# The softmax's division moved into the product that turns the probabilities

## The reference, cut to what matters

```python
s_loc = jnp.einsum('bnqkgd,bskd->bkgnqs', qb, kw).astype(jnp.float32) * scale
s_ctx = jnp.einsum('bnqkgd,bskd->bkgnqs', qb, ck).astype(jnp.float32) * scale
...
p = jax.nn.softmax(jnp.concatenate([s_loc, s_ctx, sc], axis=-1), axis=-1).astype(v.dtype)
o = (jnp.einsum('bkgnqs,bskd->bnqkgd', p[..., :3 * B_BLOCK], vw)
     + jnp.einsum('bkgnqs,bskd->bnqkgd', p[..., 3 * B_BLOCK:3 * B_BLOCK + Lc], cv))
```

## Time and profile before

| | |
|---|---|
| median of 3 runs | 2546.1 us (2545.37 to 2546.45) |
| the profiled execution: its time | 2541.14 us |
| its span, first to last instruction | 2539.3 us |
| busy: PE, DVE, ACT, POOL | 2006.7, 1748.4, 945.2, 938.2 us |
| granted TensorE clock, mean | 0.929 of full |

### The profile page before, as it was taken

The page is one execution under the profiler, slowest core; times in us unless marked ns, Lnnn a source line. Parts: engine busy times, 40 slices in busy tenths (PEclk is TensorE's granted clock), DMA queues, the critical chain, the costliest instruction groups (busy, mean ns, idle before and its releaser), DMA issues. The chain is left out here.

```text
span 2539.3 us, 27322 instructions
## 1 busy us (share of the span) xinstructions
PE 2006.7 (79%) x6925; PEld 1101.4 (43%) x6925; DVE 1748.4 (69%) x3969; ACT 945.2 (37%) x2456; POOL 938.2 (37%) x774
## 2 busy tenths in 40 slices
PE   6978897966677798778698776887778887687876
PEld 2667844755566543366454222322223222232222
DVE  2732277886776678767787777777777777777764
ACT  1402144223343434312332444444444444344443
POOL 0020022232222122202233554656545666456654
PEclk9998998987888899889899998999999999999999
DMA  8844677851111498859798999999999999999997
GB/s 318 291 150 170 227 297 294 328 209 67 67 67 67 159 339 328 325 217 402 271 367 323 422 421 393 419 422 422 421 400 412 422 422 421 410 406 422 422 421 327
DMA packets 113299, 805.53 MB, mean 317 GB/s; under 512 B 12596, under 2 KB 14006, under 8 KB 17046
## 3 DMA queue, kind: packets, MB, share of 16 engines
q0 software_dynamic: 93760, 680.96, 66.7%
q1 hardware_dynamic: 17704, 118.17, 12.6%
q10 hardware_dynamic: 1712, 4.98, 0.5%
HBM read 800.79 MB, written 3.28 MB: 317 GB/s over the span
## 5 line engine op out<-in xcount | busy, mean ns | idle before, releaser
L1201 POOL DMA_INDIRECT RG<-in_uv,idxs x264 | 351.2, 1330 | 568.0 <-DVE pl L1428 328.0
L945 ACT ACTIVATE agel<-apre 128x1 f32<-128x1 f32 x640 | 129.2, 202 | 990.3 <-DVE apre L1400 987.2
L590 PE MATMUL pl<-RG,BP 128*128 128x512 f32 x576 | 294.0, 636 | 106.7 <-ACT BP L961 106.0
L590 PE MATMUL pl<-RING,BP 128*128 128x512 f32 x576 | 282.2, 621 | 62.2 <-ACT BP L961 60.8
L615 PE MATMUL pa<-HL,RING 128*128 128x512 f32 (+2 forms) x960 | 315.5, 487 | 8.5 <-DVEq L447 8.1
L1400 DVE CUSTOM_DVE_ANT_0 R<-RG,AB 128x1024 f32<-128x1024 f32 x201 | 246.7, 1230 | 101.9 <-DMA RG<-in_uv,idxs 81.9
L1201 POOL DMA_INDIRECT RING<-in_uv,idxs x168 | 253.3, 1508 | 155.7 <-PE pl L590 68.6
L1400 DVE CUSTOM_DVE_ANT_0 R<-RING,AB 128x1024 f32<-128x1024 f32 x168 | 205.9, 1226 | 95.0 <-DMA RING<-in_uv,idxs 78.1
L615 PEld LDWEIGHTS pa<-HL,RING 128*128 128x128 f32 x960 | 166.3, 196 | 149.8 <-issue 119.1
L590 PEld LDWEIGHTS pl<-RG,BP 128*128 128x128 f32 x576 | 99.8, 192 | 294.0 <-ACT BP L961 220.1
L961 ACT ACTIVATE BP<-CT,wexp 128x128 f32<-128x128 f32 x480 | 192.7, 401 | 53.4 <-PE pl L590 15.9
(11 more groups left out here) (277 smaller groups left out, 3133.8 us busy)
## 6 DMA issues: line engine op xcount, KB each, us to landing
RING<-in_in_slabs SPq DMA_DIRECT2D x42, 1024.0 KB, 5.2
RING<-in_pq_slabs SPq DMA_DIRECT2D x24, 1152.0 KB, 5.5
RING<-in_ada_slabs SPq DMA_DIRECT2D x16, 1024.0 KB, 5.2
RING<-in_out_slabs SPq DMA_DIRECT2D x12, 1024.0 KB, 5.6
RG<-in_col_slabs POOLq DMA_DIRECT2D x8, 1024.0 KB, 6.9
RING<-in_o_slabs SPq DMA_DIRECT2D x8, 1024.0 KB, 5.6
RG<-in_uv,idxs POOLq DMA_INDIRECT x297, 12.3
RING<-in_uv,idxs POOLq DMA_INDIRECT x168, 14.5
```

Of the source, the lines that this page charges most:

```text
L590: last = nc.tensor.matmul(acc[:, c * 512:(c + 1) * 512], DG[:, k % 2, :], bufs[k % len(bufs)][:, D + c * 512:D + (c + 1) * 512], start=Fal ...
L945: A(agel[:, par, k:k + 1], apre[:, par, k:k + 1], ACT.Gelu).then_inc(gel_done, 1)
L1201: nc.gpsimd.indirect_dma_start(out=bufs[b], out_offset=None, in_=uv, in_offset=bass.IndirectOffsetOnAxis(ap=idxs[:, par, k:k + 1], axis=0) ...
```

## The change

`norm` no longer scales the probabilities. It writes a diagonal matrix, 1/total on the diagonal, into a new tile `DGN` (two deep), by scaling `ident` row by row. `turn_p` multiplies the unscaled probabilities, still the stationary operand, with this diagonal in place of the transpose with `ident`: an ordinary fp32 matmul. Before DGN's buffer is written again, `norm` waits until `turn_p` of two heads before is done.

```diff
         SMX, PTX = [view(R1, 0, 3, 640), view(RW_, AT1, 3, 640)], [view(R1, 2048, 2, 640), view(RW_, AT2, 2, 640)]
+        DGN = [view(R1, 3328, 2, P), view(RW_, AT2 + 2048, 2, P)]
...
                 for c, _ in key_blocks(t):
-                    last = tr(ps[:, c:c + P], SMX[t > 0][:, n % 3, c:c + P])
+                    last = mm(ps[:, c:c + P], SMX[t > 0][:, n % 3, c:c + P], DGN[t > 0][:, n % 2, :])
                 finish(("pT", n), last)
...
                 t = HEADS[n][0]
-                lo, hi = score_span(t)
-                p = SMX[t > 0][:, n % 3, lo:hi]
                 total = ast[:, 80 + n:81 + n]
                 dve.wait_ge(p_ready, n + 1)
                 step(V.tensor_tensor(total, total, ast[:, 120 + n:121 + n], ALU.add))
                 step(V.reciprocal(total, total))
-                step(V.tensor_scalar(p, p, total, None, ALU.mult), pn_ready)
+                if n >= 2:
+                    wait_full(dve, ("pT", n - 2))
+                step(V.tensor_scalar(DGN[t > 0][:, n % 2, :], ident, total, None, ALU.mult), pn_ready)
```

## The result

The changed kernel is slower: 2560.07 us (median of 6 runs, 2554.67 to 2565.82) against 2545.73 us for the kernel before on the same chip, 14.3 us more by the medians. The profiled execution took 2565.82 us and lies 5.7 us above its own median, so single spans have to be compared with care.

The account below looks back on a forecast made before the run. No engine is full: a loop of waits between PE and DVE bounds the attention stretches. Latents +10.0 and context +1.6 give +11.6 us, less 1 for the clock: +10.6 on the median 2546.1, forecast 2556.7 us, range 2549.5 to 2563.

Parts of the forecast that it names:

- The new wait: In DVE's norm: the wait for turn_p of two heads before, always already issued and ended by PE; zero us.
- Cost zero: The forecast's price for norm's added wait on DVE, since PE has always ended that turn_p by then.
- the stages without attention keep their lengths: Forecast sign in the profile after: stages without attention, the gather-bound one included, stay as long as before.
- DVE's product: In norm: 128 columns at 288 ns instead of 640 or 512 saves 8.0 us of DVE's time in the latents.
- PE's blocks: In turn_p: a block costs 0.108 us more at full clock, 0.19 to 0.2 us more at half.
- What of it is on the path: Latents in the merged part: 10.96 us where PE decides, +1.0 nearly level, -2.0 where DVE decides; net +10.0 us.
- by about as much: Forecast sign: DVE's waits for PE grow about as much as the merged part, which gets some 10 us longer.
- Context: Context tile's attention, PE's closed chain at 1.2 GHz: +0.27 us a head for six heads, +1.6 us.
- The clock rises: Rival: real products bring 2.4 GHz in the context's chain and half the cold turns; +4 us, time 2550; chance 0.18.
- Nothing is covered: Rival: all 152 blocks lie on PE's path, DVE's saving lost; +22 us, time 2568; chance, dearer blocks included, 0.10.
- Faster: Rival: a block costs PE no more than a transpose; time 2538 to 2544; chance 0.07, no-effect case included.
- The new wait binds: Rival: norm is held until turn_p of two heads before; still 2557 us; chance next to none.

Follow-up runs that it names:

- e9: The changed kernel with only 2 of its 38 added waits, those that no other wait implies; ratio to the kernel before 1.0029 (1.0012 to 1.0046).
- e8: The kernel before with always-fulfilled waits added to DVE's list at the same 38 places; ratio 1.0051 (1.0034 to 1.0067).
- e10: The changed kernel with 41 more instructions, fulfilled waits in DVE's list in the context tile's mix; ratio to the kernel before 1.0113 (1.0093 to 1.0133).
- e7: The kernel before with the scaling of the probabilities moved from DVE to ACT, transposes kept, DVE's list 40 shorter; ratio 1.0012 (0.9997 to 1.0027).
- e15: The kernel before with 128 instructions added to DVE's list, all fulfilled waits; ratio 1.0003 (0.9984 to 1.0022).
- e3: The changed kernel with the old transpose on PE; DVE's new norm and wait kept, division left out of the result; ratio to before 1.0016 (0.9997 to 1.0034).
- e2: The changed kernel with the old norm on DVE; PE turns blocks by a real matmul with the unit matrix; ratio to before 1.0031 (1.0011 to 1.0051).
- e1: The changed kernel measured again, nothing altered; ratio to the kernel before 1.0064 (1.0040 to 1.0088).
- e12: e9 with each latent block turned twice, the same product written again; ratio to the kernel before 1.0116 (1.0087 to 1.0144).

## Why the prediction was right, and where it was not

The direction and the size were right (2560.07 us measured, 2556.7 forecast), but they came about differently: about 11 of the 17 us come from something that the prediction had put at nothing, and what was left of the term on PE's path is some 6 us by the middle of the measurements, where 10.0 had been forecast. That the two errors have opposite signs, so that the sum came out near, is luck. Without the 11 us, as in e9 (1.0029), the time would have been some 2553 us, slower and inside the range too, for the reasons that the prediction gave.

**The new wait.** "Cost zero" is the step that failed. As a wait it was right: none of the 40 products is held by it. As 38 instructions in DVE's list it costs 11 us, since it moves tile 4's loop from 23 to 61 modulo 128. e8 has the cost with no change at all, e9 has the change without the cost, e10 and e7 put it at other tiles, and e15 makes it go away by adding more. With this falls the line "the stages without attention keep their lengths".

**DVE's product.** 286 ns were measured, 288 forecast. Of the 8.0 us of busy time 7.5 were there, and e3 shows how much they are worth when PE keeps its transposes: a merged part 7 us below the mean of the unchanged ones, and 0.16% in all where the gather stage alone would give 0.4%. The prediction gave 2 us to it. What is left of it beside the longer blocks is too small to be read: e2 (1.0031) and e9 (1.0029), without and with it, can't be told apart, but their intervals would also hide some 6 us; the merged part is 322.4 us without it and 320.2 on average with it, 2 us less, which is what was forecast and also within the scatter.

**PE's blocks.** The price of a block was forecast as 0.248 us at full clock and 0.445 at half. Measured are 1.28 to 1.31 us for five and 1.06 to 1.09 for four, so 0.26 to 0.27, and 2.40 for five and 1.98 for four at half clock, so 0.48 to 0.50. A head of four or five blocks adds 0.50 or 0.61 us at full clock (forecast 0.43 and 0.54), and 0.96 or 1.17 at half (forecast 0.77 and 1.0): 13 to 25% more. The factor of four that the Trainium skill gives for fp32 in transpose mode ("TensorE: Matmul & The Clock Gate", section Terms) is not what this kernel shows between a product and a transpose: 0.26 against 0.14 us is 1.8 to 1.9 times.

**What of it is on the path.** +10.0 us were forecast for the latents. The merged part of the changed kernel and of e1, e9 and e10 is 320.2 us on average, the five unchanged ones 316.5: +4 us, or 8 against the one profile of before, and +5.4 by DVE's account above. e9's total, with the context in it, is 7.4 us (3 to 12), so some 6 are left for the latents (1.5 to 10). All of these lie below the forecast though the blocks were dearer than forecast, but the scatter reaches up to it, so that the term was too large is likely and not shown. Part of it may be the clock: the mean granted clock of the merged part is 0.84, 0.84, 0.81, 0.83 and 0.84 in the unchanged kernels and 0.86, 0.85, 0.85 and 0.87 in the four with the whole change. But it is 0.85 also in e3 and e7, which keep the transposes, and in the changed kernel 9 of the 32 turns run wholly at half clock, as many as before. So real products are not shown to be what raises it, and how many us the rise is worth is not measured. Neither is how many of the turns counted as PE's DVE would have decided. The forecast that DVE's waits grow "by about as much" as the part was wrong in itself: where PE decides, DVE's saving is turned into waiting too, so 10 us more of time would have meant 18 more of waits. 12.9 were measured, which is 7.5 + 5.4.

**Context.** +1.6 us forecast, +1.6 in each of the eight kernels that have it. Six of its turns are in the closed chain, as in this timeline of PE in the changed kernel:

```profile
206.25 0.79 PE L616 MATMUL pa<-HG 64*128 64x128 f32 x2
206.97 0.79 PE L616 MATMUL pa<-R 128*128 128x128 f32 x2
207.69 0.69 PE L616 MATMUL po<-R,BP 128*64 128x128 f32 x2
208.31 0.79 PE L616 MATMUL pa<-HG 64*128 64x128 f32 x2
```

The turn takes 0.72 us in all of them, where it took 0.40 to 0.50, and the head shown 2.06 us instead of 1.74.

**The rivals.** *The clock rises*: in the context it does not, its clock is 0.50 before and after though the turns are real products. By the Trainium skill ("TensorE: Matmul & The Clock Gate", "Part 4: PE-mode transpose") transposes don't count as PE-busy in the way that matmuls do; this chain stays at half clock without any transpose, so it wasn't they alone that kept it there. In the merged part the mean clock rises by 0.02 to 0.03, which may be a part of the missing 4 to 6 us and is not shown to come from the real products. The argument against this rival was in part misread: of the eight turns at half clock that it names, four follow an idle PE of 3 us or more (584, 613, 649, 678), the others one of 0 to 1.6 us. *Nothing is covered*: not so, has its like at 760 us, and e12 shows it from the other side. *Faster*: no, a block costs 0.26 us at full clock. *The new wait binds*: not as a wait. A fifth way, that added instructions move a loop, was not among them.

Still open: where the slow positions begin and end (60, 61, 69 and 81 are slow, 40 and 90 are not); whether the period is 128 or a multiple of it (256 would need two slow stretches, one at 69 and one at 188 to 209; 32 is excluded, since 61 is slow and 29 isn't); and why a loop that is fetched again stops DVE twice for 4.65 us and not at each packet.

## What to carry to other kernels

Count what an edit adds to an engine's list of instructions, waits included, and look whether it shifts loops further down: a difference in a stage that the edit doesn't touch, with idle time put down to issue and more packets on an instruction queue, was the sign of it here, and a pad of waits that are always fulfilled told it apart in one run (e8). Drop waits that another wait implies. A transpose made into a product for the sake of the division can pay only where DVE, not PE, closes the loop: here 7.5 us less on DVE were bought with more work on PE that costs 8 us by itself (e2), and the two together still lose 7 (e9).

## What the runs showed of the hardware

- A further wait before an instruction that already waits became an instruction of its own: 38 waits made 38 instructions more. Of waits in a row on the same semaphore about every second one is left: 41 of 90 (e10), 90 of 188 (e15).
- DVE's instructions come in packets of 8.2 KB (0.60 MB in 73), and 128 more instructions were one packet more (74). A loop of 306 instructions is fetched once or on every pass, by where it starts modulo 128 instructions (slow at 60, 61, 69, 81); the second costs 11 to 12 us for three passes, +5 to +6 packets on each later pass, in a tile of 324 us.
- An fp32 product of 128 x 128 with a diagonal takes 0.26 to 0.27 us at 2.4 GHz and 0.48 to 0.50 at 1.2 GHz, a transpose of the same block 0.14 and 0.25.
- Without any change to its code the merged part of this kernel scatters from 312.7 to 323.1 us between profiles, while the gather stage repeats within 2.3 us (1152.4 to 1154.7).
